# A fused two-block transformer kernel: seven weight chunks split by subtraction, and a fourth output tile begun before the last unit of the first three

## The reference, cut to what matters

```python
def first_block(x, ...):                       # one layer
    z = rms_norm(x) @ w_in                     # glu, q, k, v, gates
    y_a = silu(rms_norm(causal_depthwise_conv(a_val * sigmoid(a_gate)))) @ w_conv_out
    y_b = dilated_window_attention(q, k, v) @ w_attn_out      # 16 heads of 64
    x = x + (g_a * y_a + g_b * y_b) @ w_out
    u = causal_depthwise_conv(rms_norm(x) @ w_up)             # 2 x 2816 wide
    return x + (silu(u_gate) * u_val) @ w_down

def second_block(x, ...):                      # two layers
    # layer 0, sparse: q, k, v, g and an index (qi: 8 heads of 64, ki: 64, wi: 8)
    score = sum_h(relu(qi_h @ ki.T) * wi_h)    # the 128 best keys of each row are kept
    x = layer_norm(ALPHA * x + (attention_over_kept_keys * silu(g)) @ w_out_a)
    # layer 1, stick-breaking: softplus of the logits, summed from the right, exp, times v
    x = layer_norm(ALPHA * x + (stick_breaking_attention * silu(g)) @ w_out_b)
```

## Time and profile before

| | us |
|---|---|
| median of 3 runs | 1630.21 |
| lowest, highest | 1626.49, 1630.28 |
| the profiled execution | 1634.27 |
| its span in the trace | 1632.5 |
| PE busy in it | 1540.5 (94%) |
| mean granted TensorE clock | 0.977 of full |

### The profile page before, as it was taken

The page is one execution under the profiler, slowest core; times in us unless marked ns, Lnnn a source line. Parts: engine busy times, 40 slices in busy tenths (PEclk is TensorE's granted clock), DMA queues, the critical chain, the costliest instruction groups (busy, mean ns, idle before and its releaser), DMA issues.

```text
span 1632.5 us, 21698 instructions
## 1 busy us (share of the span) xinstructions
PE 1540.5 (94%) x7740; PEld 1306.9 (80%) x7740; DVE 1153.0 (71%) x2064; ACT 877.3 (54%) x1495; POOL 692.5 (42%) x683
## 2 busy tenths in 40 slices
PE   7999898999999999999999899998899999999986
PEld 5888798797878888888888678877777878888866
DVE  4999987996463778448637358966775817888876
ACT  5444577676442444334324365577777536676642
POOL 1332243333354555545554421244443226567443
PEclk8999999999999999999999999999999999999998
DMA  6888646656332322222222568775566855555451
GB/s 205 208 185 202 160 115 140 152 139 147 116 104 90 103 91 94 101 95 99 99 95 88 151 154 193 186 164 134 132 159 156 192 114 136 127 119 131 113 116 53
DMA packets 69083, 218.60 MB, mean 134 GB/s; under 512 B 9008, under 2 KB 11568, under 8 KB 68976
## 3 DMA queue, kind: packets, MB, share of 16 engines
q1 hardware_dynamic: 48960, 144.34, 27.1%
q0 software_dynamic: 20016, 72.88, 25.4%
HBM read 203.42 MB, written 2.10 MB: 126 GB/s over the span
## 4 chain that ended last, share of the span: by engine, by line
PE 69%; DVE 12%; ACT 8%; DMA 6%; issue 2%; POOL 1%; SPq 1%; ACTq 0%; DVEq 0%; POOLq 0%
PE bank L358 68%; DMA k_both<-k_both 2%; PE bank L364 2%; DVE r L397 2%; DMA w_raw<-in_weights 2%; DMA w_lo<-in_weights 1%; ACT w_hi L368 1%; DVE score L1824 1%; DVE small L1819 1%; ACT soft L368 1%; ACT w_lo L368 1%; ACT prob L368 1%; DVE ext L397 1%; DVE sp_lo L385 1%; DVE pt_lo L385 1%
## 5 line engine op out<-in xcount | busy, mean ns | idle before, releaser
L358 PE MATMUL bank<-x_hi,w_hi 128*128 128x512 f32 x872 | 350.5, 402 | 17.0 <-ACT w_hi L368 6.7
L368 ACT ACTIVATE w_hi<-w_raw 128x1024 fp32r<-128x1024 f32 (+2 forms) x206 | 213.7, 1039 | 277.8 <-PE bank L358 261.0
L404 POOL TENSOR_TENSOR w_lo<-w_raw,w_hi 128x512 fp32r<-128x512 f32 (+1 forms) x179 | 256.3, 1453 | 239.0 <-ACT w_hi L368 239.0
L358 PE MATMUL bank<-x_hi,w_lo 128*128 128x512 f32 x872 | 344.5, 395 | 10.7 <-DMA w_lo<-in_weights 10.7
L358 PE MATMUL bank<-x_lo,w_hi 128*128 128x512 f32 x872 | 343.8, 394 | 0.0
L607 POOL DMA_DIRECT2D w_lo<-in_weights x139 | 122.5, 886 | 308.0 <-ACT w_lo L368 274.1
L358 PEld LDWEIGHTS bank<-x_hi,w_hi 128*128 128x128 f32 x872 | 166.3, 191 | 51.7 <-ACT w_hi L368 7.5
L358 PEld LDWEIGHTS bank<-x_hi,w_lo 128*128 128x128 f32 x872 | 166.0, 190 | 48.6 <-DMA w_lo<-in_weights 12.5
L358 PEld LDWEIGHTS bank<-x_lo,w_hi 128*128 128x128 f32 x872 | 166.5, 191 | 30.7
L358 PE MATMUL bank<-a_hi,w_hi 128*128 128x512 f32 x416 | 162.0, 389 | 0.0
L358 PE MATMUL bank<-a_hi,w_lo 128*128 128x512 f32 x416 | 161.8, 389 | 0.0
(11 more groups left out here) (219 smaller groups left out, 3334.6 us busy)
## 6 DMA issues: line engine op xcount, KB each, us to landing
w_raw<-in_weights SPq DMA_DIRECT2D x223, 512.0 KB, 3.8
w_lo<-in_weights POOLq DMA_DIRECT2D x139, 512.0 KB, 6.9
k_both<-k_both SPq DMA_DIRECT2D x48, 128.0 KB, 5.4
turned<-raw SPq DMA_DIRECT2D x74, 64.0 KB, 2.5
alibi<-in_alibi SPq DMA_DIRECT2D x16, 256.0 KB, 4.3
w_raw<-in_weights SPq DMA_DIRECT2D x8, 384.0 KB, 3.0
r<-in_x SPq DMA_DIRECT2D x8, 256.0 KB, 7.0
r<-in_x SPq DMA_DIRECT2D x4, 512.0 KB, 6.4
```

The source lines that it names most:

```text
L358: return e.matmul(out, lhsT, rhs, start=start, stop=stop, skip_group_check=resumed)
L368: return self.act.run(lambda e: e.activation(out, in_, func, **kw), after, 0.07 + size(out) * 0.00086 + 0.09 * len(kw))
L404: return self.pool.run(lambda e: e.tensor_tensor(out, a, b, op), after, cost)
```

## The change

Two parts. First, kiwi, qi 0 to 3 and the value chunks ("vb", 0) and ("vb", 4) of the stick mixer go to `subtract`; these two are the first two of that stage. Second, in each mixer a second `late` tile: slices 0 to 6 of output tile 3 are run ahead of slice 7 of tiles 0 to 2, once all 16 heads are in PE's list and the heads' banks are not pending. It takes its bank from the heads' ones, so the ring grows to five (seven in the stick mixer); the index stage sets it back to three. Tile 3 is then gone from the plain `tiles` call behind.

```diff
-SUBTRACTED = ("attn_out", "conv_out", "out", "val", "upgate", "down")
+SUBTRACTED = ("attn_out", "conv_out", "out", "val", "upgate", "down", "kiwi", "qi")
+SUBTRACTED_VALUES = (("vb", 0), ("vb", 4))
...
-            if self.plan[c][0] in SUBTRACTED:
+            if self.plan[c][0] in SUBTRACTED or self.plan[c] in SUBTRACTED_VALUES:
...
-        for key in late:
-            while not may():
+        for n, key in enumerate(late):
+            while not may(n):
...
+    def may_begin(self, n):
+
+        if n and (self.n_heads < HEADS or any(b.pending for b in self.sbank)):
+            return False
+        self.ring = self.psum[0:3 + 2 * n]
+        return True
...
-                                      self.attn_evict, KT, self.os_ready, [("attn_out", 2)], lambda: True)
+                                      self.attn_evict, KT, self.os_ready, [("attn_out", 2), ("attn_out", 3)], self.may_begin)
...
-        for _ in self.tiles([("attn_out", c) for c in range(3, KT)], self.h, self.hl, lambda k: o_ready[k], self.attn_evict):
+        for _ in self.tiles([("attn_out", c) for c in range(4, KT)], self.h, self.hl, lambda k: o_ready[k], self.attn_evict):
...
         keys = [("kiwi", 0)] + [("qi", c) for c in range(4)]
+        self.ring = self.psum[0:3]
...
-                                      lambda k: self.got(self.os_ready, k), self.mix_evict, KT, self.os_ready, [("out_a", 2)], lambda: True)
+                                      lambda k: self.got(self.os_ready, k), self.mix_evict, KT, self.os_ready, [("out_a", 2), ("out_a", 3)], self.may_begin)
...
-        for _ in self.tiles([(name, c) for c in range(3, first)], hi, lo, lambda k: os_ready[k], self.mix_evict):
+        for _ in self.tiles([(name, c) for c in range(4, first)], hi, lo, lambda k: os_ready[k], self.mix_evict):
...
-        def last_head():
-
-            if self.n_heads < HEADS - 1 or any(b.pending for b in self.z_banks[0]):
+        def last_head(n):
+
+            if self.n_heads < HEADS - 1 + n or any(b.pending for b in self.z_banks[0] + n * self.z_banks[1][1:]):
                 return False
-            self.ring = self.psum[0:5]
+            self.ring = self.psum[0:5] + n * self.psum[6:8]
             return True
...
-                                      lambda k: self.got(self.os_ready, k), self.mix_evict, KT, self.os_ready, [("out_b", 2)], last_head)
+                                      lambda k: self.got(self.os_ready, k), self.mix_evict, KT, self.os_ready, [("out_b", 2), ("out_b", 3)], last_head)
```

## The result

| | before | changed |
|---|---|---|
| median of 6 runs, us | 1630.73 | 1644.14 |
| lowest, highest | 1626.49, 1636.60 | 1637.53, 1649.10 |
| span of the profiled execution | 1632.5 | 1647.3 |

What follows compares the result with a forecast made beforehand. The prediction took PE, busy 94% of the span, to bound the kernel. Its terms, 4.0 - 4.3 - 4.9 - 5.5 = -10.7 us, took 1630.2 to 1619.5 us, with a range of 1610 to 1628.

Steps and rivals of the forecast that it cites:

- Step 1: End of the first mixer: tile 3 early delays column sums and spread, opening new PE idle; +4.0 us, bounds +2.7 and +4.4.
- Step 2: Start of the index stage: subtracted chunks remove PE's waits for kiwi and qi 0, -8.4 us; va 0's wait grows, +2.3.
- Step 3: First sparse head: PE waits 1.8 us, 18 dense matmuls move into the heads; with Step 2 -4.3, bounds -2.6 and -8.4.
- Step 4: Sparse mixer's end and vb: tile covers slice 7's wait, subtracted values shorten vb's supply; -4.9 us, bounds -2.5 and -6.8.
- Step 5: End of the stick mixer: early tile 3 removes the last o_lo wait and the half clock behind it; -5.5 us.
- 6. five banks: From attn_out to the feed-forward: PE is busy 438 of 438 us there, so 0.
- Rival (c): Sparse heads: PE early at every head, each adding 1.8 us of wait; slower, +5.5 us, 1635.7; chance 0.05.
- (d): Sparse and stick mixers' ends: early tile does nothing, its weights not there in turn; -3.3 us, 1626.9; chance 0.2 with another rival.

Runs made afterwards that it cites:

- e7: Only output tile 3 of the first mixer begun early, with its ring of five, against the kernel before: 1636.26 us, 1.0034.
- e1: Only the index part, kiwi and qi 0 to 3 subtracted, against the kernel before: 1641.64 us, 1.0053.
- e6: vb 0 and vb 4 subtracted and the sparse mixer's output tile 3 begun early, against the kernel before: 1635.02 us, 1.0016.
- e4: Only output tile 3 of the stick mixer begun early, against the kernel before: 1629.32 us, 0.9968.
- e2: e1 with 116 units (348 dense matmuls) required in PE's list ahead of the first head's scores: 1623.24 us, 0.9928 of the kernel before.
- e12: e2 with 112 units in place of 116, plus vb 0 and vb 4 subtracted and the stick mixer's tile 3 early: 1619.27 us, 0.9916 of before.
- e9: The kernel before with one number changed, 264 units instead of 280 dealt to the sparse heads, nothing subtracted: 1664.05 us, 1.0187.
- e3: Only vb 0 and vb 4 subtracted, against the kernel before: 1629.10 us, 0.9981.
- e11: e2 plus vb 0, 1, 4 and 5 subtracted and the stick mixer's tile 3 early: 1618.66 us, 0.9919 of the kernel before.

## Why the prediction was wrong, step by step

| step | forecast | in the changed kernel | alone |
|---|---|---|---|
| 1. first mixer's tile | +4.0 | +4.8 | +4.7 (e7) |
| 2 and 3. index, choice, heads | -4.3 | +10.6 (-7.9, -5.1, +23.6) | +8.0 (e1: -7.4, -6.4, +21.8) |
| 4. sparse end and vb | -4.9 | +2.5 | +0.3 (e6) |
| 5. stick end | -5.5 | -5.7 | -5.7 (e4) |
| 6. five banks | 0 | 0 | 0 (e7) |

**Step 1** was right in place, sign and size: sums at 451.0 (forecast 450.7), two idles of 1.80 and 2.19 (some 2 us each), the spread at 457.0 (456.8), and a low clock behind them (0.50 in 457 to 461).

**Step 2** was right in itself. PE's waits for kiwi and qi 0 are gone but for 0.58 us, the clock is full in 929 to 945, and the stretch gains 7.9 us against 8.4 (va 0's wait lies behind its end). The new place of va 0's DMA cost less than worked out: a wait of 1.92 us instead of 1.41, not 3.7. The reason is the transfers of the rotation that it stands behind: I had taken 4.8 us for them to land, and they took 2.0 (the last was issued at 951.05 and the product with sin started at 953.1). The DMA itself took 8.25 us, not 7.25. The wait was followed by some 3.4 us of low clock all the same.

**Step 3** is the one that failed. It had PE 1.8 us early at the first head, -2.6 as the worst bound of the two steps even with a half clock, and the heads otherwise as they were. Two terms were wrong.

The first is the price of coming early. I saw 30 dense matmuls leave the stretch ahead of the first head and priced 18 x 0.227; all 30, 6.8 us, went into the heads. PE waited 3.76 us there and not 1.8, then 4.12 at the third head, and the first three lots took 11.2 us more, at a granted clock of 0.80. With the cover given back (e2, e12) or never taken (e9) they take as long as before, within 0.6.

The second is the heads' lots, which the prediction had at nothing: "more dense work lies between them now, not less". The lists said otherwise, and it could be read before any run: 9 for 30, 15 for 27, in front of heads where the trace of before has 5.0 and 3.4 us of idle. These two lots take 8.0 us more. That they do so because they are thin is argued and not shown: in e9 15 and 15 cost 0.6, and PE might also be early there from the first head on.

Most of the 15 us between forecast and measurement of steps 2 and 3 lie in these two. Rival (c) named the heads as the place and PE's earliness as the mechanism, and was given 0.05; PE was early as (c) says, but for three lots and the two thinned ones, not at every head. That the deal of the list makes the loss is shown by e1 and e2: the same subtractions with the list filled first are 18 us faster. e9 adds that other lots without any subtraction can cost 32 us, by a wait of another kind.

**Step 4** put the gain of both edits under one bound, the supply of vb, and had -4.9 for the two together. The subtracted values alone give that number in vb's stretch (e3), with the 2.05 ahead of slice 7 still there. Adding the tile removes those 2.05, opens 2.9 ahead of vb and takes the gain away: +0.3 in e6, +2.5 in the changed kernel. I had asked what is late next behind vb, but not behind slice 7: the tile takes 21 matmuls from under the layer norm's chain there. This is the step 1 argument, sums and spread with too little between them, which I had made for the first mixer and left out for the second.

The prediction weighed, and set aside, the rule of the Trainium skill (GPSIMD Engine Reference, section "1. Specifications") that POOL shares its SBUF interfaces with VectorE. The trace agrees: in the changed kernel DVE's additions of 0.41 us take up to 1.51, and of 0.68 up to 1.78, beside POOL's subtractions and additions, 6.3 us more in sum than before. What such time costs is set by the slack: nothing in e3, and in e11, with four chunks subtracted, a wait of 3.24 us ahead of vb. Beside the tile its share stays open.

**Step 5** was right in place and size, in every run that has the tile. The prediction's (d), that the tile does nothing there, came in none of them.

In the whole, -10.7 was forecast and the profile gives +13.8 up to the last output matmul. The places that failed are steps 2 and 3 together with 14.9 and step 4 with 7.4; the remaining 2 are steps 1 and 5 and the stretches up to 402 and 1577, which scatter by that much.

## What to carry to other kernels

Where a planner deals filler work, a saving upstream changes the deal everywhere behind it: count the filler between each pair of waits before and after, and hold the counts against the idle that the trace has at just those waits. Count also how much filler is left ahead of the first chain that the engine will wait for. The same subtractions kept 8 us or lost 10 by the deal alone. A tile begun early is taken from under whatever ran beside it later, so ask of each such move what chain (a norm's sums and spread) loses its cover; at the stick mixer's end it was a clear gain, 5.7 us, and in the two places where PE's next work hangs on a norm it wasn't.

## What the runs showed of the hardware

Behind 1.92 us of idle at 962.6 the granted clock fell for 3.4 us (0.61 on average from 962.6 to 966.0), where behind 2.05 at 1252 and 1.51 at 452 it had stayed full: the length of the last idle doesn't decide by itself, as the prediction had used it. And how much executions of the same list differ goes by place: up to 402 us, where no list differs, the traces lie 6.7 us apart, and in the sparse heads 10.6, with other counts of low clock. One profile can't tell a change of 5 us in the heads from none.
